# A two-part transformer program on one Trainium2 core, without the matmuls whose result nobody reads

## The reference, cut to what matters

```python
def rms_norm(x, w):
    x32 = x.astype(jnp.float32)
    y = x32 * lax.rsqrt(jnp.mean(x32 * x32, axis=-1, keepdims=True) + EPS)
    return (y * w.astype(jnp.float32)).astype(x.dtype)

def swiglu_ffn(h, w_gate_up, w_down):
    gate, up = jnp.split(h @ w_gate_up, 2, axis=-1)
    return (jax.nn.silu(gate) * up) @ w_down
...
def second_block(x, c, ctx, c_ctx, mod_w, mod_b, norm_g, ...):
    for i in range(DEPTH):
        update_ctx = i < DEPTH - 1
        sh_l, sc_l, g_l = modulation(c, mod_w[i], mod_b[i])
        ...
        h_lat = rms_norm_2(x_lat, norm_g[i]) * (1.0 + sc_l[:, None, :]) + sh_l[:, None, :]
        ...
        x_lat = x_lat + g_l[:, None, :] * y_lat
        if update_ctx:
            x_ctx = x_ctx + g_c * y_ctx
    return rms_norm_2(x_lat, final_g)
```

## Time and profile before

| | us |
|---|---|
| median of 3 runs | 2533.63 |
| lowest, highest of them | 2533.34, 2536.1 |
| profiled execution, its own time | 2532.86 |
| span of that execution | 2531.0 |
| PE busy | 2445.4 (97%) |
| DVE busy | 1679.5 (66%) |
| ACT busy | 1106.6 (44%) |
| DMA queues 1 and 10, share of the 16 engines' span | 21.8%, 5.2% |

### The profile page before, as it was taken

The page is one execution under the profiler, slowest core; times in us unless marked ns, Lnnn a source line. Parts: engine busy times, 40 slices in busy tenths (PEclk is TensorE's granted clock), DMA queues, the critical chain, the costliest instruction groups (busy, mean ns, idle before and its releaser), DMA issues.

```text
span 2531.0 us, 37056 instructions
## 1 busy us (share of the span) xinstructions
PE 2445.4 (97%) x14414; PEld 1983.8 (78%) x14414; DVE 1679.5 (66%) x3270; ACT 1106.6 (44%) x2069; POOL 0.2 (0%) x4
## 2 busy tenths in 40 slices
PE   8998999999999999989999999999999999999998
PEld 6877898778888778788987888888866666788666
DVE  6767576474447875675865544488586676599774
ACT  4345355443322343454544432323446676232573
POOL 0000000000000000000000000000000000000000
PEclk9999999999999999999999999999999999999999
DMA  4320142223337422202412323563210001132311
GB/s 156 92 75 27 43 147 87 67 84 100 95 112 233 151 89 83 74 4 75 147 63 67 107 93 100 176 218 117 67 34 18 18 18 34 50 93 68 85 49 51
DMA packets 74093, 219.29 MB, mean 87 GB/s; under 512 B 21312, under 2 KB 21568, under 8 KB 73152
## 3 DMA queue, kind: packets, MB, share of 16 engines
q1 hardware_dynamic: 48384, 176.06, 21.8%
q10 hardware_dynamic: 25536, 40.87, 5.2%
HBM read 214.80 MB, written 2.10 MB: 86 GB/s over the span
## 4 chain that ended last, share of the span: by engine, by line
PE 85%; DVE 8%; ACT 4%; issue 2%; ACTq 0%; DMA 0%; DVEq 0%
PE bank L602 21%; PE bank L603 20%; PE bank L604 20%; PE bank L843 4%; PE bank L879 4%; PE bank L853 3%; DVE w_lo L564 2%; PE bank L633 1%; PE bank L634 1%; PE bank L635 1%; ACT w_hi L557 1%; PE bank L659 1%; PE bank L660 1%; PE bank L661 1%; PE bank L1455 1%
## 5 line engine op out<-in xcount | busy, mean ns | idle before, releaser
L557 ACT ACTIVATE w_hi<-w_raw 128x1024 fp32r<-128x1024 f32 x334 | 353.8, 1061 | 562.0 <-PE bank L604 516.2
L564 DVE TENSOR_TENSOR w_lo<-w_raw,w_hi 128x1024 fp32r<-128x1024 f32 x334 | 407.8, 1222 | 231.0 <-ACT w_hi L557 230.0
L602 PE MATMUL bank<-a_hi,w_hi 128*128 128x512 f32 x1344 | 534.5, 398 | 20.2 <-DVE w_lo L564 18.2
L604 PE MATMUL bank<-a_hi,w_lo 128*128 128x512 f32 x1344 | 525.6, 391 | 0.0
L603 PE MATMUL bank<-a_lo,w_hi 128*128 128x512 f32 x1344 | 525.2, 391 | 0.0
L602 PEld LDWEIGHTS bank<-a_hi,w_hi 128*128 128x128 f32 x1344 | 252.0, 188 | 82.5 <-issue 18.5
L604 PEld LDWEIGHTS bank<-a_hi,w_lo 128*128 128x128 f32 x1344 | 251.7, 187 | 55.5
L603 PEld LDWEIGHTS bank<-a_lo,w_hi 128*128 128x128 f32 x1344 | 252.2, 188 | 51.7 <-issue 1.0
L602 PE MATMUL bank<-b_hi,w_hi 128*128 128x512 f32 x440 | 182.5, 415 | 4.0 <-DVE w_lo L564 2.7
L603 PE MATMUL bank<-b_lo,w_hi 128*128 128x512 f32 x440 | 172.7, 393 | 0.0
L604 PE MATMUL bank<-b_hi,w_lo 128*128 128x512 f32 x440 | 172.3, 392 | 0.0
(11 more groups left out here) (462 smaller groups left out, 4510.6 us busy)
## 6 DMA issues: line engine op xcount, KB each, us to landing
w_raw<-w_tiles SPq DMA_DIRECT2D x334, 512.0 KB, 3.5
mod_raw<-mod_tiles ACTq DMA_DIRECT2D x48, 512.0 KB, 4.3
d_bias<-rpb_rows ACTq DMA_DIRECT2D x16, 224.0 KB, 4.6
hT<-xT ACTq DMA_DIRECT2D x8, 256.0 KB, 5.7
m_in<-memT ACTq DMA_DIRECT2D x2, 1024.0 KB, 4.9
mod_cond<-cond_rows ACTq DMA_DIRECT2D x2, 1024.0 KB, 5.9
out<-hT ACTq DMA_DIRECT2D x8, 256.0 KB, 2.2
ctx_sq<-ctxT ACTq DMA_DIRECT2D x1, 1024.0 KB, 7.7
```

The source lines that it names most:

```text
L557: act.activation(w_hi[:, t % SPLIT, :], w_raw[:, t % RAW, :], ACT.Copy).then_inc(sem("w_rounded"), 1)
L564: dve.tensor_tensor(w_lo[:, t % SPLIT, :], w_raw[:, t % RAW, :], w_hi[:, t % SPLIT, :].bitcast(f32), ALU.subtract).then_inc(sem("w_split"), 1)
L602: pe.matmul(o, wh, chunk(hi, k, n), start=k == 0, stop=False)
L604: mm = pe.matmul(o, wl, chunk(hi, k, n), start=False, stop=k == kc - 1)
```

## The change

All calls of `warm_pe` and the function itself are deleted. Nothing takes their place.

```diff
@@ -1292,13 +1292,6 @@
-        def warm_pe(pe, n, *key):
-
-            b = claim(pe, "warm", *key)
-            for _ in range(n):
-                mm = pe.matmul(b[:, :], ident, con[:, 0:512], start=True, stop=True)
-            mm.then_inc(*freed("warm", *key))
-
@@ -2679,13 +2672,10 @@
             even_out_pe(pe)
-            warm_pe(pe, 2, "m2", 1)
             ssq_pe(pe, ("m2", 1, "lat"), S)
             ctx_ssq_pe(pe, 1)
-            warm_pe(pe, 1, "m2_rstd", 1)
             rstd_pe(pe, ("m2", 1, "lat"), S)
             ctx_rstd_pe(pe, 1)
-            warm_pe(pe, 1, "odd_in")
             odd_in_pe(pe)
@@ -2698,9 +2688,7 @@
-            warm_pe(pe, 1, "final_sq")
             last_ssq_pe(pe, ("final",))
-            warm_pe(pe, 1, "final")
             rstd_pe(pe, ("final",), S)
@@ -3244,14 +3232,10 @@
                 last_ssq_pe(pe, ("x_post", l))
-                warm_pe(pe, 1, "x_rstd", l)
                 rstd_pe(pe, ("x_post", l), S)
-                warm_pe(pe, 2, "f", l)
                 ffn_pe(pe, l)
                 last_ssq_pe(pe, ("f_post", l))
-                warm_pe(pe, 1, "f_rstd", l)
                 rstd_pe(pe, ("f_post", l), S)
-                warm_pe(pe, 2, "mix", l + 1)
             second_pe(pe)
```

## The result

The changed kernel took 2543.32 us (median of 6 runs, 2540.96 to 2545.04) where before took 2533.49 (6 runs, 2530.18 to 2536.1) on the same chip: a ratio of 1.0038, 95% interval 1.0028 to 1.0049. It is slower by 9.8 us, beyond the forecast range, whose upper end was 2539.2, and near the number of rival C. The profiled execution took 2544.42 us.

The account below looks back on a forecast made before the run. PE was taken as the bound, with matmuls in it for 97% of the span. From the profiled 2532.86 us, boundaries 0, end -0.4 and clock drops +3.2 gave 2535.7, stated as 2535.6 us; range 2532.3 to 2539.2.

Parts of the forecast that it names:

- rival C: At the five boundaries: longer low-clock stretches, clearly slower, 2543.7 us if all paid twice, deciding from 2538.7; chance 0.14.
- the chosen case: At every stage boundary the clock falls once each, giving 2534.5 to 2537.5 us; chance 0.60.
- PE waits at the boundaries, the deleted work is in that wait: At five stage boundaries the deleted matmuls lie in PE's wait for ACT and DVE, so removal directly wins 0.
- The end wins 0.4 us: At the program's end the chain runs through both deleted matmuls: -0.4 us, bounds 0 and -0.6.
- I take the drop as nearly certain: Behind boundary gaps grown to 3.9 us TensorE's clock drops; two new drops at 1.6 us each, +3.2 us.
- The boundary's own length stays: At the boundaries DVE's scaling stays directly behind the weight split, at the same distance from the last product: 0 us.
- rival E: At five boundaries transposes run at lower clock, 0.44 us longer each, outlasting DVE's split: 2538 us; chance 0.03.
- The rest at nothing: Elsewhere, bank claims, DMA, semaphores, other engines' instructions and the weight stream cost nothing: 0 us.
- The sum: Whole kernel: 2532.86 + 0 - 0.4 + 3.2 = 2535.7 us, stated as 2535.6, 2.0 us above the median before.
- B: At the boundaries drops grow neither in number nor cost, only the end changes: 2532.5 to 2533.2 us; chance 0.21.
- D: Freed PE time is on the path after all, clearly faster, needing 5.1 of 15.5 us; chance 0.02.
- The rule of the Trainium skill: Between matmul bursts: keep gaps short or the clock halves; taken strictly, all five boundaries lose it, costing 7.6 us.

## Why the prediction was wrong

The direction and the mechanism of the chosen case held: slower, by TensorE's clock, and nothing won at the boundaries. The size did not, and with it the range and the chance of a clear loss.

- *PE waits at the boundaries, the deleted work is in that wait.* Right. The first product still waits for ACT.
- *The end wins 0.4 us.* Right, 0.39, in three profiles of three.
- *"I take the drop as nearly certain. Then the profiled execution gains two drops: + 2 x 1.6 = +3.2 us."* This is the step that failed. Its first half is right: all five stages were below full clock in all three profiles of the changed kernel. The price is the term that was mis-sized. I took 1.6 us from a gap of 2.2 us, where the low stretch over dense work costs what 3.2 us at half the clock would. With the gap at 3.8 us it is on for 4.7 us of dense work and costs 2.2 to 2.3, whether it is 10.2 us long or 6.8 (18.79 us at the first boundary of the third profile). And I counted only the two stages that had been clean, while the three with a drop rose too, by 0.7, 0.6 and 0.3. Stages alone: 2.2 + 0.7 + 2.3 + 0.6 + 0.3 = 6.2 us with their second digits, in the first pair of profiles, not 3.2.
- *The boundary's own length stays.* Wrong by 1.1 us: 0.2 at each of three, where the transposes ran at the lower level and outlasted the split (rival E, which took 0.44 us for each), and 0.6 at the odd mixer.
- *The rest at nothing.* Wrong by 1.7 us, in the last stretch, in three profiles of three.
- *The sum.* 6.2 + 1.1 - 0.4 + 1.7 = 8.6 us, inside the two intervals of the time (7 to 12 and 7 to 14 us). The rest of the first profiles' 11.6 us lies in code that is the same: ahead of the first boundary the changed one is 3.1 us longer, with 13.7 us of low stretches there instead of 6.8.
- *Rivals.* C named the place and the way, that the boundary without its fill is one long stretch at the lower level, with a time of 2543.7 us where 2543.3 was measured. That is partly luck: its doubled price is 3.2 a boundary, and the boundaries gave 7 us and not 11. B and D fell. I gave C 0.14 although its row stood in the profile, because I weighed how often a drop comes and not how long it stays.
- *The rule of the Trainium skill* (page "TensorE: Matmul & The Clock Gate", section "Why this matters for your kernels") is to leave no long idle gaps between bursts of matmuls. With this case's 1.6 us for a drop it gave 7.6 us, nearer to the result than my sum. The trace still disagrees on the short gaps, since three of five drop in every profile of before; on the wide gaps it agrees, five of five.

## What to carry to other kernels

Matmuls whose result nobody reads are free here as long as they lie in a wait that another engine sets, and what they buy shows in the stage behind the wait, not in their own rows: compare that stage at granted clock 1.00 with the same stage below. Price such a change at every boundary, those with a drop already included, and by how long the low clock can lie over the dense work behind the wait (3.4 us gave 1.6, 4.7 gave 2.2 here). Before taking the fill out, try the other direction: fill until about 0.5 us of idle time is left, and no more. A fill that is caught by the lower clock takes twice as long and can outlast the wait, as at the odd mixer. Where runs of one kernel are 12 us apart, compare the lengths of stages in profiles, and the low clock outside them, before calling a few microseconds an effect.

## What the runs showed of the hardware

- 36 records of 4 columns in place of 512 did as little for the clock as none: 0.982 in both, against 0.992.
- Where in a boundary the clock falls decides the cost. With a low stretch of 3.4 us over the fill the stage took 16.62 us, with one of 6.8 us that began in the last idle stretch 19.00.
- An idle stretch of 2.2 us was followed by a drop in one place or execution and not in another: the same first stage took 16.61 us in two profiles of before and 18.16 in one.
- Identical code ran in 2526.8 to 2538.7 us on one chip, a spread of 12 us. The code outside the boundaries took 2092 to 2101 us in six profiles, in the order of the low clock in it (20.5 to 34.1 us).
- Drops come far from any edit: the low stretch near 2483.6 us, in all three profiles of the changed kernel, stands 270 us behind the start of the odd mixer's stage.
